# Summing and turning the modulation chunks four at a time in two projection stages

## The chip, the cores and the metric

One core of a Trainium2 chip runs the whole program. The metric is the device time of one execution in microseconds (us), as a median of several executions. TensorE is PE in the rows (its weight loads PEld), VectorE DVE, ScalarE ACT, GpSimd POOL, SyncE SP.

## What is computed

A two-layer network over 512 latent and 256 context rows of width 1024, followed by a second block; all in float32. Only the modulation matters here: for each layer a vector of six times 1024 numbers, once for the latent condition and once for the context condition, which shifts and scales the normalised rows and gates the two residual sums.

```python
silu_c = jax.nn.silu(c)
silu_cc = jax.nn.silu(c_ctx)
for i in range(DEPTH):
    ...
    sh1l, sc1l, g1l, sh2l, sc2l, g2l = [m[:, None, :] for m in jnp.split(silu_c @ ada_w[i] + ada_b[i], 6, axis=-1)]
    sh1c, sc1c, g1c, sh2c, sc2c, g2c = jnp.split(silu_cc @ ada_w[i] + ada_b[i], 6, axis=-1)
    h_lat = rmsnorm(x, norm1_w[i]) * (1.0 + sc1l) + sh1l
    h_ctx = rmsnorm(ctx, norm1_w[i]) * (1.0 + sc1c) + sh1c
    ...
    x = x + g1l * o_lat
```

## The kernel before

The program is a row of stages; each stage is a block that all engines enter and leave together, so a stage begins when the last engine of the one before is done. Weights come in chunks of 1024 x 512 through a ring of three slots, loaded by SP in a fixed order; SP waits for a slot to be free before it issues the next load. Every large product is made from a high and a low part of each operand (three matmuls, all at line 608); POOL and ACT cut the weights into these parts (lines 127, 128, 134).

The modulation is 24 chunks of 512 columns (12 for each layer). Four of them belong to `prologue`, 12 are spread over `ssd_project` and 8 over `project_qkv`. The class `Modulate` handles one chunk `i` at a time, with one PSUM bank for the products and one for all that follows:

- `products` (line 440, PE): the two condition vectors, padded to 32 columns, times the chunk. Eight matmuls of 32 columns; the k-th goes to column group k mod 4, that is to PSUM partitions 0, 32, 64 or 96, so that four groups hold partial sums. It waits for `copied` of the chunk before.
- `copy` (line 448, ACT): PSUM bank to SBUF (`part`).
- `sums` (line 454, PE): one matmul with `pick`, a 128 x 2 matrix of ones in the right rows, adds the four partial rows to two rows.
- `add` (line 461, DVE): adds the bias to the two rows (2 x 512).
- `turn` (line 468, PE): four transposes of 2 x 128.
- `file` (lines 479 and 483, DVE): copies the turned columns to `modc` if the chunk is one that is used as columns; for a scale also 1 + and times the norm weight.
- `store` (line 490, SP): at the stage's end the rows of chunks in `keep` go to DRAM.

`prepare` (lines 420 to 425, POOL) makes the padded conditions and `pick` at the stage's start; `start` (line 416, SP) loads the biases. In `ssd_project` the order on PE is written by hand: for n = 0 to 3 (the z part) four blocks b of 36 matmuls, with `products(n)` after b = 1, `sums(n)` after b = 2, `turn(n)` after b = 3; then 32 passes f (the x part), each of 48 matmuls and, from f = 1 to 24, six transposes of the pass before (line 955), with `products`, `sums` and `turn` of chunk 4 + f // 4 after passes f with f mod 4 = 1, 2, 3. A pass goes on to ACT (copy, line 1015), DVE (convolution, lines 1070 and 1074), ACT (silu, lines 1022 and 1023), PE (the transposes of line 955, behind the matmuls of the next pass) and DVE again (`file(f)` of the stage, lines 1055 and 1056).

In `project_qkv` PE does j = 0, 1, 2 (keys and values, first and second half of the queries) of four blocks b each, and then turns twelve tiles (`turn(n)`, lines 2996 and 2999); the modulation steps stand between these. DVE does norm and rotation of each part (`scale`, lines 3090 to 3102, and `rope`, lines 3112 to 3115) with the modulation's `add` and `file` between them, for instance

```python
            x = q[:, :, 0:HALF]
            scale(1, x, NL, 8, NT + NL)
            mod.file(dve, 2)
            rope(x, 0, 8, 0)
            rope(x, 0, 8, 1)
            mod.add(dve, 3)
```

## Time and profile before

| | us |
|---|---|
| median of 3 runs | 3552.27 |
| lowest, highest | 3546.49, 3552.39 |
| span of the profiled execution | 3548.8 |
| PE busy in it | 3138.1 (88%) |
| DVE, ACT, POOL busy in it | 1363.9, 986.9, 822.8 |
| `ssd_project`, first to last of PE's matmuls at line 608 | 69 to 547 |
| `project_qkv` | 1613.5 to 1735 |

The profiled execution has no time of its own but its span; the median stands 3.5 us above that span. The profile's page gives busy times over the whole span, so what a change in one stage is worth has to be read from that stage's own rows: start to start of neighbouring instructions on the engine that never idles, and the waits in square brackets.

### The profile page before, as it was taken

The page shows a single profiled execution, that of the slowest core. Times are in us where ns is not written, and L with a number is a line of the kernel's source. Part 1 is how long each engine was busy: PE and PEld are TensorE (multiplying, and loading weights), DVE is VectorE, ACT ScalarE, POOL GpSimd, SP SyncE. Part 2 cuts the span into 40 slices and gives each one's busy share as a digit, 9 for nine tenths or more (in the row PEclk, how much of TensorE's full clock was granted, in tenths as well). Part 3 has the DMA queues.
Part 4 walks back from the last instruction along what each step waited for, and adds up shares of the span by engine and source line. Part 5 has one row for each costly group of instructions (what it writes and reads, how often), then busy time and mean ns, then how long its engine had stood idle before and what let it go on. Part 6 is the DMA issues. An engine that isn't in the chain of part 4 may idle for free. (4 is left out here: it accounts for less than half of the span.)

```text
span 3548.8 us, 41092 instructions
## 1 busy us (share of the span) xinstructions
PE 3138.1 (88%) x16301; PEld 1978.1 (56%) x16301; DVE 1363.9 (38%) x2165; ACT 986.9 (28%) x2224; POOL 822.8 (23%) x574
## 2 busy tenths in 40 slices
PE   5999997878969999968899698887998996879998
PEld 3778885656723333326567233333776645668877
DVE  2128876774331111114664321113637743233311
ACT  3112225654132221223353211111343302332211
POOL 3333324660001101113101000000533101434432
PEclk8999999998979999989999799999999998899999
DMA  6444454433099999962303899998123133132231
GB/s 224 147 150 136 156 182 153 149 96 136 5 372 395 396 402 395 400 235 100 141 1 125 324 401 412 416 411 342 57 85 109 63 134 110 48 119 93 69 129 42
DMA packets 272074, 697.21 MB, mean 196 GB/s; under 512 B 16032, under 2 KB 62972, under 8 KB 269580
## 3 DMA queue, kind: packets, MB, share of 16 engines
q1 hardware_dynamic: 263104, 672.35, 50.2%
q0 software_dynamic: 6656, 16.78, 2.0%
q10 hardware_dynamic: 2124, 5.46, 0.4%
q8 instruction: 130, 2.13, 0.3%
q14 instruction: 60, 0.49, 0.0%
HBM read 647.30 MB, written 47.25 MB: 196 GB/s over the span
## 5 line engine op out<-in xcount | busy, mean ns | idle before, releaser
L608 PE MATMUL ps<-h_parts,weights_high 128*128 128x512 f32 (+3 forms) x2560 | 745.7, 377 | 29.1 <-PEq L258 17.6
L134 POOL TENSOR_TENSOR weights_low<-ring,weights_high 128x1024 fp32r<-128x1024 f32 (+1 forms) x205 | 499.1, 2438 | 712.0 <-ACT weights_high L127 701.9
L608 PEld LDWEIGHTS ps<-h_parts,weights_high 128*128 128x128 f32 (+2 forms) x2560 | 466.3, 190 | 139.1 <-POOL weights_low L134 26.6
L608 PE MATMUL ps<-h_parts,weights_low 128*128 128x512 f32 (+2 forms) x1280 | 479.5, 375 | 0.0
L1989 PE MATMUL ps<-area 128*32 128x512 f32 (+1 forms) x1632 | 285.9, 597 | 2.6 <-ACT area L2077 2.5
L608 PEld LDWEIGHTS ps<-h_parts,weights_low 128*128 128x128 f32 (+1 forms) x1280 | 242.5, 189 | 47.0 <-issue 0.8
L127 ACT ACTIVATE weights_high<-ring 128x1024 fp32r<-128x1024 f32 (+1 forms) x138 | 143.8, 1051 | 252.4 <-PE ps L608 233.3
L2187 PE MATMUL ps<-area 128*64 128x512 f32 x832 | 190.2, 610 | 20.0 <-ACT area L2267 7.0
L608 PE MATMUL ps<-weights_high,h_parts 128*128 128x512 f32 x608 | 197.6, 400 | 7.1 <-PEq L258 7.1
L1989 PEld LDWEIGHTS ps<-area 128*32 128x32 f32 (+1 forms) x1632 | 84.0, 124 | 189.1 <-issue 186.4
L1074 DVE SCALAR_TENSOR_TENSOR area<-area,param_columns 128x772 f32<-128x772 f32 x128 | 184.2, 1439 | 10.0 <-issue 0.4
L1989 PE MATMUL ps<-ring,area 128*32 128x512 f32 (+1 forms) x864 | 155.4, 595 | 0.1
L2187 PEld LDWEIGHTS ps<-area 128*64 128x64 f32 x832 | 69.6, 140 | 132.2 <-issue 130.6
L608 PEld LDWEIGHTS ps<-weights_high,h_parts 128*128 128x128 f32 x608 | 115.0, 189 | 47.2 <-issue 20.1
L1975 POOL DMA_INDIRECT summed_rows<-area,picked_half_rows x16 | 25.1, 1569 | 480.1 <-DVE area L2114 480.1
L608 PE MATMUL ps<-weights_high,y_parts 128*128 128x512 f32 x384 | 122.2, 398 | 6.9 <-DVE weights_low L1655 6.9
L608 PE MATMUL ps<-weights_low,h_parts 128*128 128x512 f32 x304 | 120.4, 396 | 0.0
L608 PE MATMUL ps<-weights_high,hidden_parts 128*128 128x512 f32 x352 | 112.5, 400 | 7.2 <-POOL weights_low L134 7.2
L2187 PE MATMUL ps<-ring,area 128*64 128x512 f32 x432 | 102.2, 620 | 18.0 <-DMA ring<-in_moe_w 5.8
L148 POOL CAST weights_high<-ring 128x1024 fp32r<-128x1024 f32 x18 | 20.6, 1147 | 410.6 <-DVE area L758 192.9
L1262 ACT ACTIVATE weight_parts<-ps,area 128x128 f32<-128x128 f32 x384 | 104.4, 391 | 32.4 <-PE ps L1189 32.1
L128 POOL CAST weights_high<-ring 128x1024 fp32r<-128x1024 f32 (+1 forms) x49 | 50.7, 1034 | 268.6 <-PE ps L608 268.4
(449 smaller groups left out, 4786.8 us busy)
## 6 DMA issues: line engine op xcount, KB each, us to landing
area<-in_moe_w SPq DMA_DIRECT2D x103, 2048.0 KB, 24.6
ring<-in_moe_w SPq DMA_DIRECT2D x54, 2048.0 KB, 25.4
weight_parts<-in_moe_w SPq DMA_DIRECT2D x35, 2048.0 KB, 24.6
ring<-in_ada_w SPq DMA_DIRECT2D x24, 2048.0 KB, 8.4
ring<-in_ssd_in_w SPq DMA_DIRECT2D x12, 2048.0 KB, 7.9
ring<-in_w_in SPq DMA_DIRECT2D x11, 2048.0 KB, 7.9
ring<-in_w_ffn_in SPq DMA_DIRECT2D x10, 2048.0 KB, 7.7
area<-x_dram SPq DMA_DIRECT2D x12, 1024.0 KB, 5.0
```

The lines of the kernel that those rows point to most:

```text
L127: return eng.activation(hi, src, ACT.Copy)
L128: return eng.tensor_copy(hi, src)
L134: pool.tensor_tensor(lo, views[k][:, ks, cols], hi, ALU.subtract).then_inc(self.low_p, 1)
L148: pool.tensor_copy(self.part(self.hi, m, ks, cols), src[:, ks, cols])
L608: mm = pe.matmul(out, a, b, start=start and n == 0, stop=stop and n == 2)
L1074: last = dve.scalar_tensor_tensor(c, pad[:, f % 2, j:j + width], col(env, "ssd_conv_w", j * 32 + f), c, ALU.mult, ALU.add)
L1262: last = act.activation(ex[:, u % 3, d, h * P:(h + 1) * P], spread_at(u, d)[:, h * P:(h + 1) * P], ACT.Exp, bias=nacum[:, c, hh:hh + 1])
L1975: pool.indirect_dma_start(out=halves, out_offset=at(env.spots, e), in_=y[e % 2], in_offset=None, compute_op=ALU.add).then_inc(added, 16)
L1989: mm = pe.matmul(ps[i * n:(i + 1) * n, bank, :], x, w, start=first, stop=last, skip_group_check=True)
L2187: mm = pe.matmul(ps[i * L:(i + 1) * L, bank, :], x, w, start=first, stop=last, skip_group_check=True)
```

## The change

A new class `ModulateFours` takes the place of `Modulate` in `ssd_project` (12 chunks, three fours) and `project_qkv` (8 chunks, two fours). `products` is as before. `copy` puts the four chunks of a four side by side into a buffer of 4 x 512. `sums` works on a four: `pick` is padded to 32 columns and four matmuls put the sums of the four chunks at PSUM partitions 0, 32, 64 and 96 of one bank. `add` is one instruction of 128 x 512, `turn` four transposes of 128 x 128, and `file` picks the columns of all four chunks. Since only two of each 32 rows carry values, POOL clears the whole row buffer first, and SP's bias loads (and whatever SP has behind them) wait for that. Of the 16 row stores 8 are left: `keep` is (2, 5) in place of (2, 3, 4, 5). The places of the steps move too, and in `project_qkv` `prepare` moves to the front of POOL's work. `prologue` keeps the old class.

```diff
+class ModulateFours:
+    def start(self, sp):
+        sp.wait_ge(self.cleared, 1)
+        for i, (layer, c) in enumerate(self.chunks):
+            sp.dma_start(self.place(i), self.env.ins["ada_b"][layer, c * HALF:(c + 1) * HALF]
...
+    def prepare(self, pool):
+        pool.memset(self.rows, 0.0).then_inc(self.cleared, 1)
+        pool.memset(self.cond, 0.0)
+        pool.memset(self.pick, 0.0)
+        pool.drain()
+        pool.tensor_copy(self.cond[:, :, 0:2], self.env.cond[:])
+        for j in range(4):
+            pool.tensor_tensor(self.pick[:, 0:2], self.pick[:, 0:2], self.env.ident[:, 32 * j:32 * j + 2], ALU.add)
+            pool.drain()
...
+    def copy(self, act, i):
+        act.wait_ge(self.env.mod_used, self.m0 + i + 1)
+        if i >= 4:
+            act.wait_ge(self.summed, i // 4)
+        act.activation(self.part[:, i % 4, :], self.env.ps[:, self.banks[0], :], ACT.Copy).then_inc(self.copied, 1)
+
+    def sums(self, pe, b):
+        if b >= 1:
+            pe.wait_ge(self.filed, b)
+        pe.wait_ge(self.copied, 4 * b + 4)
+        for j in range(4):
+            mm = pe.matmul(self.env.ps[32 * j:32 * j + 32, self.banks[1], :], self.pick, self.part[:, j, :], start=True, stop=True,
+                           skip_group_check=True)
+        mm.then_inc(self.summed, 1)
...
+    def turn(self, pe, b):
+        pe.wait_ge(self.added, b + 1)
+        for j in range(4):
+            s = slice(j * P, (j + 1) * P)
+            tr = pe.transpose(self.env.ps[:, self.banks[1], s], self.rows[:, b, s], self.env.ident[:])
+        tr.then_inc(self.turned, 1)
...
@@ ssd_project
-        mod = Modulate(env, st, [(0, c) for c in range(4, 12)] + [(1, c) for c in range(4)], (6, 7), keep=(2, 3, 4, 5))
+        mod = ModulateFours(env, st, [(0, c) for c in range(4, 12)] + [(1, c) for c in range(4)], (6, 7), keep=(2, 5))
...
-                    elif b == 2:
-                        mod.sums(pe, n)
-                    elif b == 3:
-                        mod.turn(pe, n)
+            mod.sums(pe, 0)
...
+                if f == 0:
+                    mod.turn(pe, 0)
                 if n < mod.n:
                     if f % 4 == 1:
                         mod.products(pe, n, at[n])
-                    elif f % 4 == 2:
-                        mod.sums(pe, n)
-                    elif f % 4 == 3:
-                        mod.turn(pe, n)
+                    elif f % 16 == 14:
+                        mod.sums(pe, n // 4)
+                    elif f % 16 == 15:
+                        mod.turn(pe, n // 4)
...
-            for n in range(nz):
-                mod.add(dve, n)
-                mod.file(dve, n)
+            mod.add(dve, 0)
+            mod.file(dve, 0)
...
@@ project_qkv
-                if m == CUTS:
+                if m == ahead:
                     mod.prepare(pool)
...
-                    if j >= 1 and b % 2 == 0:
-                        mod.sums(pe, 2 * j - 2 + b // 2)
+                    if (j, b) == (2, 2):
+                        mod.sums(pe, 0)
                     if b % 2 == 1 and j + b > 1:
-                        if j >= 1:
-                            mod.turn(pe, 2 * j - 2 + b // 2)
                         mod.products(pe, 2 * j - 1 + b // 2, at_mod[2 * j - 1 + b // 2])
```

PE at the end of `project_qkv`, from the last `turn` inside the loop over j to the end of the stage. Before (468 is `turn` of a chunk, 454 `sums`, 440 `products`, 2996 and 2999 the stage's own turns):

```order
L468 MATMUL ps<-identity,area 128x2 x4
L440 MATMUL ps<-ring,area 32x512 x8
L2996 MATMUL ps<-identity,area 64x128 x24
L454 MATMUL ps<-area 2x512
...
L468 MATMUL ps<-identity,area 128x2 x4
L440 MATMUL ps<-ring,area 32x512 x8
L454 MATMUL ps<-area 2x512
L468 MATMUL ps<-identity,area 128x2 x4
L2999 MATMUL ps<-identity,area 128x128 x16
```

After (551 is `products`, 566 `sums` of a four, 582 `turn` of a four, 3111 and 3114 the stage's own turns):

```order
L551 MATMUL ps<-ring,area 32x512 x8
L3111 MATMUL ps<-identity,area 64x128 x24
L582 MATMUL ps<-identity,area 128x128 x4
...
L3114 MATMUL ps<-identity,area 128x128 x8
L551 MATMUL ps<-ring,area 32x512 x8
L3114 MATMUL ps<-identity,area 128x128 x8
L566 MATMUL ps<-area 32x512 x4
L3114 MATMUL ps<-identity,area 128x128 x8
L582 MATMUL ps<-identity,area 128x128 x4
```

The last two chunks' chains of products, sums and turn no longer stand ahead of the last four of the stage's own turns; the second four is summed and turned between and behind them.

DVE in `project_qkv`, from the first scaling of the second half of the queries on. Before (461 is `add`, 479 and 483 `file`, 3102 the scaling, 3112 the first step of a rotation):

```order
L3090 TENSOR_TENSOR area<-area 128x2048
...
L461 TENSOR_TENSOR area<-ps,area 2x512
...
L3102 TENSOR_TENSOR area<-area 128x512 x4
L479 COPY modulation_columns<-ps 128x2x4
L483 SCALAR_TENSOR_TENSOR modulation_columns<-modulation_columns,param_columns 128x2x4
L3112 TENSOR_TENSOR area<-area 128x256 x4
```

After (575 is `add`, 596 the copy in `file`, 3075 the copy of a turned tile):

```order
L575 TENSOR_TENSOR area<-ps,area 128x512
L3204 TENSOR_TENSOR area<-area 128x2048
...
L3215 TENSOR_TENSOR area<-area 128x512 x4
L3225 TENSOR_TENSOR area<-area 128x256 x4
...
L596 COPY modulation_columns<-ps 128x2x4 x2
L3075 COPY area<-ps 128x512
L575 TENSOR_TENSOR area<-ps,area 128x512
```

One `add` stands ahead of the last scaling, and no modulation step is left between it and the last rotation.

POOL at the start of `ssd_project`, ahead of its first cut of weights. Before:

```order
L420 MEMSET area 128x256
L421 COPY area<-identity 128x2
L423 COPY area<-conditions 128x8x2
L425 TENSOR_TENSOR area<-area,identity 128x2 x3
L128 CAST weights_high<-ring 128x512
```

After:

```order
L530 MEMSET area 128x1536
L531 MEMSET area 128x256
L532 MEMSET area 128x32
L534 COPY area<-conditions 128x8x2
L536 TENSOR_TENSOR area<-area,identity 128x2 x4
L128 CAST weights_high<-ring 128x512
```

A clearing of 1536 columns, one of 32 and a fourth addition come in ahead of the first cut; a copy of two columns goes.

## Rows read from the trace of the kernel before

**Rows 1.** The page's first line.
```profile
span 3548.8 us, 41092 instructions
```

**Rows 2.** Windows: PE, PEld, DVE, ACT, POOL busy; granted clock; DMA share; GB/s.
```profile
69.00:547.00 478.00, 476.67 (x2573) 377.24 (x2574) 258.12 (x243) 84.94 (x169) 168.88 (x96) 0.99 0.46 156
1613.50:1709.80 96.30, 95.75 (x440) 67.30 (x440) 41.11 (x83) 21.38 (x30) 27.59 (x16) 0.98 0.44 156
1709.80:1735.00 25.20, 20.59 (x204) 11.58 (x201) 19.23 (x42) 9.11 (x16) 0.00 (x0) 1.00 0.69 252
```

**Rows 3.** Timeline of PE in the z part: products; one chunk's sums between matmuls.
```profile
97.16 1.92 PE L440 MATMUL ps<-ring,area 128*32 128x512 f32 x16
...
107.02 0.40 PE L608 MATMUL ps<-weights_low,h_parts 128*128 128x512 f32 x1
107.25 0.40 PE L608 MATMUL ps<-weights_high,h_parts 128*128 128x512 f32 x1
107.58 1.02 PE L454 MATMUL ps<-area 128*2 128x512 f32 x2
108.53 0.50 PE L608 MATMUL ps<-weights_high,h_parts 128*128 128x512 f32 x1
108.86 0.39 PE L608 MATMUL ps<-weights_low,h_parts 128*128 128x512 f32 x1
```

**Rows 4.** Timeline of PE: first x pass; then stage transposes and a chunk's turn.
```profile
229.93 0.70 PE L608 MATMUL ps<-h_parts,weights_high 128*128 128x512 f32 x2 [0.72 <-ACT area L1007]
...
269.04 0.82 PE L955 MATMUL ps<-identity,area 128*128 128x128 f32 x6
269.79 0.41 PE L468 MATMUL ps<-identity,area 2*128 2x2 f32 x4
270.12 0.73 PE L608 MATMUL ps<-h_parts,weights_high 128*128 128x512 f32 x2
```

**Rows 5.** Clearings on POOL by form; timeline of PE at the start of `ssd_project`.
```profile
L1727 POOL MEMSET area<- 128x512 f32 x1 | 0.5, 525 | 178.5 <-POOLq L258 178.5
L420 POOL MEMSET area<- 128x256 f32 x3 | 0.9, 312 | 16.2 <-POOLq L258 16.2
...
68.96 1.11 PE L608 MATMUL ps<-h_parts,weights_high 128*64 128x512 f32 x2 [8.14 <-POOL weights_low L134]
```

**Rows 6.** Timeline: silu's second half on ACT, transposes on PE, convolution on DVE.
```profile
270.80 6.29 DVE L1074 SCALAR_TENSOR_TENSOR area<-area,param_columns 128x772 f32<-128x772 f32 x4
277.66 0.40 ACT L1023 ACTIVATE area<-area 128x256 f32<-128x256 f32 x1
278.69 0.82 PE L955 MATMUL ps<-identity,area 128*128 128x128 f32 x6
...
408.24 0.40 ACT L1023 ACTIVATE area<-area 128x256 f32<-128x256 f32 x1
408.77 0.84 PE L955 MATMUL ps<-identity,area 128*128 128x128 f32 x6
...
528.05 4.31 DVE L1074 SCALAR_TENSOR_TENSOR area<-area,param_columns 128x772 f32<-128x772 f32 x4
```

**Rows 7.** Timeline of SP at the end of `ssd_project`: the row stores.
```profile
553.77 2.44 SPq L490 DMA_DIRECT2D mod_rows_dram<-area  x8
```

**Rows 8.** Waits of DVE from 1678 to 1709 us: total, times, longest.
```profile
DVE area L461 <- PE ps L454: 7.4, 2, 3.8
DVE modulation_columns L479 <- PE ps L468: 3.7, 2, 2.6
```

**Rows 9.** Timeline of the end of `project_qkv` and the first matmul behind it.
```profile
1708.35 2.29 DVE L3090 TENSOR_TENSOR area<-area 128x2048 f32<-128x2048 f32 x1
...
1728.47 0.42 DVE L3115 TENSOR_TENSOR area<-area 128x256 f32<-128x256 f32 x1
...
1731.97 2.00 PE L2999 MATMUL ps<-identity,area 128*128 128x128 f32 x16
...
1735.02 1.42 PE L2790 MATMUL ps<-area 64*128 64x256 f32 x6 [1.05 <-PEq L258]
```

More of the change, by code:

```diff
@@ L493, in kept, with __init__, end, place @@
         sp.wait_ge(self.stored, 16 * sum(c // 2 in self.keep for _, c in self.chunks))
+class ModulateFours:
+    def __init__(self, env, st, chunks, banks, keep=()):
+        self.env, self.chunks, self.banks, self.keep = env, chunks, banks, keep
+        self.n = len(chunks)
+        self.fours = self.n // 4
+        self.cond, self.pick = st.sb("padded_conditions", [P, KD, 32]), st.sb("pick_rows", [P, 32])
+        self.part = st.sb("partial_rows", [P, 4, HALF])
+        self.rows = st.sb("mod_rows", [P, self.fours, HALF])
+        self.ready, self.bias_in, self.copied = st.sem("conditions_ready"), st.sem("bias_in"), st.sem("partials_copied")
+        self.summed, self.added, self.turned = st.sem("fours_summed"), st.sem("bias_added"), st.sem("fours_turned")
+        self.filed, self.stored, self.cleared = st.sem("columns_filed"), st.sem("mod_stored"), st.sem("rows_cleared")
+        self.m0 = env.mods
+        env.mods += self.n
+    def end(self, i):
+        self.env.ring_.ends.append([(self.env.mod_used, self.m0 + i + 1)])
+        return len(self.env.ring_.ends) - 1
+    def place(self, i):
+        return self.rows[32 * (i % 4):32 * (i % 4) + 2, i // 4, :]
+    def start(self, sp):
+        sp.wait_ge(self.cleared, 1)
+        for i, (layer, c) in enumerate(self.chunks):
+            sp.dma_start(self.place(i), self.env.ins["ada_b"][layer, c * HALF:(c + 1) * HALF]
+                         .partition_broadcast(2)).then_inc(self.bias_in, 16)
+    def prepare(self, pool):
[7 more added lines that the diff above has]
+            pool.drain()
+        pool.drain().then_inc(self.ready, 1)
+    def products(self, pe, i, k):
+        env, bank = self.env, self.banks[0]
+        if i == 0:
+            pe.wait_ge(self.ready, 1)
+        else:
+            pe.wait_ge(self.copied, i)
+        env.ring_.wait(pe, k)
+        w = env.ring_.view(k, KD, HALF)
+        for q in range(KD):
+            j = 32 * (q % 4)
+            mm = pe.matmul(env.ps[j:j + 32, bank, :], self.cond[:, q, :], w[:, q, :], start=q < 4, stop=q >= 4,
+                           skip_group_check=True)
+        mm.then_inc(env.mod_used, 1)
+    def copy(self, act, i):
[9 more added lines that the diff above has]
+            mm = pe.matmul(self.env.ps[32 * j:32 * j + 32, self.banks[1], :], self.pick, self.part[:, j, :], start=True, stop=True,
+                           skip_group_check=True)
+        mm.then_inc(self.summed, 1)
+    def add(self, dve, b):
+        if b == 0:
+            dve.wait_ge(self.bias_in, 16 * self.n)
+        dve.wait_ge(self.summed, b + 1)
+        rows = self.rows[:, b, :]
+        dve.tensor_tensor(rows, self.env.ps[:, self.banks[1], :], rows, ALU.add).then_inc(self.added, 1)
+    def turn(self, pe, b):
[4 more added lines that the diff above has]
+        tr.then_inc(self.turned, 1)
+    def file(self, dve, b):
+        env = self.env
+        dve.wait_ge(self.turned, b + 1)
+        turned = env.ps[:, self.banks[1], :].rearrange("p (k r) -> p r k", r=P)
+        for i in range(4):
+            layer, c = self.chunks[4 * b + i]
+            q = {0: 0, 1: 1, 3: 2, 4: 3}.get(c // 2)
+            if q is None:
+                continue
+            dst = env.modc[:, q, :, 4 * (c % 2):4 * (c % 2) + 4]
+            dve.tensor_copy(dst, turned[:, 32 * i:32 * i + 2, :])
+            if q in (1, 3):
+                dve.drain()
+                a = env.col_at["norm1_w" if q == 1 else "norm2_w"] + layer * KD + 4 * (c % 2)
+                dve.scalar_tensor_tensor(dst, dst, 1.0, env.cols[:, a:a + 4].unsqueeze(1).broadcast_to([P, 2, 4]), ALU.add, ALU.mult)
+        dve.drain().then_inc(self.filed, 1)
+    def store(self, sp):
+        for i, (layer, c) in enumerate(self.chunks):
+            if c // 2 in self.keep:
+                sp.wait_ge(self.added, i // 4 + 1)
+                sp.dma_start(self.env.mod_dram[layer, :, c * HALF:(c + 1) * HALF], self.place(i)).then_inc(self.stored, 16)
+    def kept(self, sp):
+        sp.wait_ge(self.stored, 16 * sum(c // 2 in self.keep for _, c in self.chunks))
@@ L1061, in _ @@
                 n = nz + f // 4
-                if f % 4 == 0 and f > 0:
-                    mod.file(dve, n - 1)
-                if f % 4 == 3:
-                    mod.add(dve, n)
+                if f % 16 == 0 and f > 0:
+                    mod.file(dve, n // 4 - 1)
+                if f % 16 == 15:
+                    mod.add(dve, n // 4)
                 dve.wait_ge(out, g0 + 2 * f + 2)
@@ L3024, in _ @@
             turn(1)
-            mod.sums(pe, 4)
+            mod.turn(pe, 0)
+            mod.products(pe, 5, at_mod[5])
             turn(2)
             turn(3)
-            mod.turn(pe, 4)
-            mod.products(pe, 5, at_mod[5])
             turn(4)
             turn(5)
-            mod.sums(pe, 5)
+            mod.products(pe, 6, at_mod[6])
             turn(6)
             turn(7)
-            mod.turn(pe, 5)
-            for i in (6, 7):
-                mod.products(pe, i, at_mod[i])
-                mod.sums(pe, i)
-                mod.turn(pe, i)
-            for n in range(8, 12):
-                turn(n)
+            mod.products(pe, 7, at_mod[7])
+            turn(8)
+            turn(9)
+            mod.sums(pe, 1)
+            turn(10)
+            turn(11)
+            mod.turn(pe, 1)
         @block.scalar
```

44 lines of the change are left out of this document (16 added, 28 removed).

## The prediction, made before the changed kernel ran

> **What bounds the kernel now.** I read the page first, then the stretches of the two changed stages, then the timeline of PE inside them, and last the other engines where PE waits. From 69 to 547 us, all of `ssd_project`'s matmuls, PE is busy 476.67 of 478.00 us at a granted clock of 0.99 [rows 2]; the next engine, DVE, is busy 258.12. So whatever is taken out of PE's row there shortens the stage, until the next chain is late. From 1613.5 to 1709.8 (`project_qkv`, the three parts) PE is again busy 95.75 of 96.30 us. Its last 25.20 us are different: PE is busy 20.59 us and DVE 19.23 [rows 2], and the last of the stage's own turns, 16 records at 1731.97, starts only when the last rotation on DVE, at 1728.47, and two chunks' chains are through [rows 9]. So that tail is bound by DVE and by hand-overs. The stages follow one another with a meeting of all engines, so I take what is won in one stage to be kept by the rest of the program.
>
> **Sums.** I read PE's timeline from start to start. Two matmuls of line 608 in a row start 0.23 us apart (107.02, 107.25); the sums start 0.33 after the matmul ahead, the next matmul 0.95 after the sums (107.58 to 108.53), and the one behind that 0.33 later again [rows 3]. So each edge costs 0.10 more than a plain step, and sums that stand alone cost 0.95 + 0.20 = 1.15 us. Where they follow other small work the edges are paid already: 0.95. What do four sums side by side cost? The row of products is the nearest: 16 records over four column groups in 1.92 us, against 2 records in 1.02 us for the single sum [rows 3]. Were nothing side by side, 16 records would take eight times the single sum, some 7.6 us. Four deep in each group fits the row, so two deep (four matmuls, 8 records) should take what one sum takes now. I use 0.95 or 1.15 for a four; the other end, nothing side by side, is 4 x 0.95 = 3.8.
>
> The Trainium skill (TensorE: Matmul & The Clock Gate, section Part 3: Packing small matmuls, row/col tiling) gives less than that: three column tiles of 32 x 512 measured 2.38 times as fast as one by one. By it, as an estimate, four sums would take about 1.25 times one; 0.24 us more for each of the five fours, 1 us in all. The products' row here is nearer to four times, and the sum goes by that row.
>
> **Turns.** Four small transposes take 0.33 us start to start (269.79 to 270.12), 0.53 when they stand alone. Six full ones take 0.75 (269.04 to 269.79), 0.125 each, so four full ones 0.50 [rows 4].
>
> **`ssd_project`, z part.** Four sums go: 4 x 1.15 = 4.6. Three turns go: 3 x 0.53 = 1.6. The fourth turn stood where PE then waited 0.72 us for ACT's last evacuation before the first x pass [rows 4]: going, it wins nothing, and the four's sums (0.95) stand in the same gap and cost nothing. Gain 6.2.
>
> **x part.** Eight sums go, six of them behind transposes: 6 x 0.95 + 2 x 1.15 = 8.0. Two fours come: 0.95 + 1.15 = 2.1. Gain 5.9. Turns: six behind transposes and one alone, 6 x 0.33 + 0.53 = 2.5; the eighth lies behind PE's last matmul and is off the path. One turn of a four comes, 0.5 (the last again off the path). Gain 2.0. The first four's turn is put behind the first pass, and DVE now files it ahead of its first convolution: turn and hand-over 0.75 us, two copies and a drain 0.5, less what ACT's copy takes anyway. PE waits there for the silu of that pass now, so the delay shows: I take a loss of 0.85, between 0 and 1.3.
>
> Is the next chain late then? PE's transposes of a pass wait for that pass's silu. In the pass after a turn, silu ended at 278.06 and PE came at 278.69, 0.6 us later; in the pass of the products 408.64 and 408.77, no more than the hand-over [rows 6]. A pass without modulation takes PE about 9.3 us, and the chain from its last matmul through copy, convolution and silu 9.0 (269.04 to 278.06 [rows 4, 6]). The slack is per pass and does not add up, so the gains stand, narrowly.
>
> **Start of the stage.** PE's first matmul at 68.96 has waited 8.14 us, at the end for POOL's first low part [rows 5]; all of `prepare` lies on that path. Clearing takes 312 ns for 256 columns and 525 for 512, so 0.83 ns a column and 1.38 us for 1536. The clearing of `pick` and the fourth addition come on top and a small copy goes; from the 312 ns of the smaller clearing I put the three at 0.2 to 0.3 together. Loss 1.6, at least the 1.38 and at most 3 if DVE's own clearing at the same time is in the way. SP's twelve bias loads wait for that clearing and the next ring load waits behind them; but that load also waits for POOL's first cut, and its slot is needed tens of us later: nothing.
>
> **End of the stage.** Eight stores take SP 2.44 us of issue behind the last feature store [rows 7]; four go. That wins up to 1.2, or nothing if the feature store lands last. I take 0.6.
>
> Stage: 6.2 + 5.9 + 2.0 - 0.85 - 1.6 + 0.6 = 12.25 us won.
>
> **`project_qkv`.** Up to the third part's evacuation four sums (1.15 each) give way to one: 3.45. The turns beside products cost 0.33 each, four of them, and one waited 0.5 more. PE's loop so ends some 4.9 us sooner. DVE can follow: between 1678 and 1709 us it waited 7.4 and 3.7 us for sums and turns of chunks [rows 8], 11.1 us that go. So the last scaling starts at 1703.45 in place of 1708.35. From there to the end of the last rotation (1728.89) DVE takes 20.54 us [rows 9]; the gaps that two adds, two files and a third add leave between its steps sum to 3.3 us, so 17.2 remain: 1720.65, 8.25 us sooner. Behind it stand two stage turns (half of the 16 records in 2.00 us, 1.0), the sums of the second four (1.0), two turns (1.0), four full transposes (0.6), two columns filed on DVE (1.2) and the meeting (0.4): 5.2 us, where before 6.1 lay between 1728.89 and the next stage's 1735.02 [rows 9]. Gain 9.1, of which I take 8.8 for hand-overs not seen. `prepare` grows to some 3.5 us and moves ahead of POOL's third cut, which PE needs about 15 us later: covered. The last ring loads go out sooner, not later.
>
> **Sum.** 12.25 + 8.8 = 21.05 us. Against the profiled span: 3548.8 [rows 1] to 3527.8. The median stands 3.5 above the span, so 3552.27 - 21.05 = 3531.2.
>
> **Rivals.**
> 1. DVE does not follow in `project_qkv`: its chain is late by something else (a ring load, ACT's queue), and only PE's 4.9 us count there. For: DVE has 11 us of waits that could hide others. Against: those waits name only sums and turns. 17.1 us won: 3535.
> 2. The change does not do what it says: the four sums run one after another. Each costs 2.85 more at five places, all but part of the first on the path: 14 us back, 7 won: 3545. Against it stands the products' row.
> 3. Slower: the convolution chain takes over in the x part. Its slack is 0.1 to 0.6 us a pass. The same four steps on DVE take 6.29 us where POOL cuts weights beside them and 4.31 where it doesn't [rows 6]. If PE's shorter passes move the cuts so that the whole chain (the first step too) is hit longer, each of 24 passes is late: at 0.9 us a pass the gain is gone, at 1.2 us the kernel takes 28.8 - 21 = 8 us more: 3560. Against: POOL starts a cut when PE ends a pass, so both move together. The Trainium skill (SBUF — State Buffer, section Who interferes with whom) says why it can happen at all: a VectorE instruction with two SBUF inputs contends with a GpSimd instruction that reads SBUF.
> 4. What is won is given back later, in a stage bound by its weight stream: 3550. Against: no load of a later stage starts before these stages end but for the ring's three slots.
>
> **Chances.** Forecast 0.72; rival 1 0.13; rival 2 0.05; rival 3 0.05; rival 4 0.05. A measurement of this kernel can tell about 0.2%, 7 us, from no change. Faster by more: 0.72 + 0.13 + a part of rival 2, 0.87; within: 0.08; slower: 0.05. Range: the lower end from the bounds (start at 1.4, first convolution hidden, end of stage 1.2, tail in full: 24 us) and 4 us of spread between runs, 3524; the upper end takes in rival 1 and the same spread, and comes near rival 2: 3543.
>
> **What would show it.** PE from its first matmul to its last in `ssd_project` shorter by about 13 us, its start 1.6 us later within the stage; a four's sums 0.95 us from start to next start; transposes of line 955's kind waiting no more than before except in the second pass; `project_qkv` 8 to 9 us shorter, with DVE's waits for sums gone; every later stage of its old length. A four's sums near 3.8 us would mean rival 2; waits of PE for silu of 0.5 us or more in most passes, rival 3.

## The result, and the profile after

The changed kernel took 3520.99 us (median of 4 runs, 3519.04 to 3523.30), beside 3551.17 (median of 4) for the kernel before on the same chip. The ratio on record is 0.9919, 95% interval 0.9906 to 0.9933; the two medians divided give 0.9915. Timed again in five rounds it took 3521.66 us beside 3549.63, with the same ratio and interval: 28.0 us faster. The prediction was 3531.2, range 3524.0 to 3543.0. The sign was right, and so was the mechanism in the two changed stages; the time lies 3 us below the range.

The page of the changed kernel, its first line and its busy row, answers to [rows 1]:

```profile
span 3521.5 us, 40919 instructions
...
PE 3112.1 (88%) x16241; PEld 1969.6 (56%) x16241; DVE 1351.5 (38%) x2150; ACT 984.0 (28%) x2224; POOL 822.0 (23%) x578
```

PE's busy time fell by 26.0 us and the span by 27.3. The windows of the two changed stages (columns as in [rows 2]) show that PE still bounds both, except in the last 20 us of `project_qkv`:

```profile
70.75:540.00 469.25, 462.95 (x2538) 374.82 (x2538) 252.60 (x240) 84.36 (x170) 169.34 (x96) 0.99 0.46 159
1595.75:1688.00 92.25, 92.22 (x440) 66.94 (x442) 43.40 (x78) 21.85 (x31) 27.07 (x18) 0.98 0.45 162
1688.00:1708.00 20.00, 16.52 (x180) 9.98 (x176) 16.90 (x41) 8.37 (x14) 0.00 (x0) 1.00 0.87 317
```

In the timeline of PE, a four's sums, at the end of the z part and behind a pass's transposes in the x part, are these (start, duration). They answer to [rows 3]:

```profile
224.49 0.40 PE L725 MATMUL ps<-weights_high,h_parts 128*128 128x512 f32 x1
224.81 1.07 PE L566 MATMUL ps<-area 128*32 128x512 f32 x8
225.98 0.70 PE L725 MATMUL ps<-h_parts,weights_high 128*128 128x512 f32 x2
...
371.35 0.82 PE L1069 MATMUL ps<-identity,area 128*128 128x128 f32 x6
372.09 1.06 PE L566 MATMUL ps<-area 128*32 128x512 f32 x8
373.09 0.73 PE L725 MATMUL ps<-h_parts,weights_high 128*128 128x512 f32 x2
```

Eight records (four sums) take 1.06 us, where one sum of two records took 1.02. Start to start it is 1.00 in the x part (372.09 to 373.09), where one sum took 0.95. So the four run side by side.

What the stretches took, from the start of one stage to the start of the next, in two profiles of the kernel before and two of the changed one:

| stretch (start in the first profile of before) | before, us | changed, us | difference of the means |
|---|---|---|---|
| setup, `prologue` (0) | 65.1, 64.9 | 65.3, 64.3 | -0.2 |
| `ssd_project` (65.1) | 492.6, 492.2 | 478.6, 478.3 | -14.0 |
| `ssd_scan` (557.6) | 274.7, 273.7 | 271.7, 271.6 | -2.5 |
| output, first MoE, norm (832.3) | 781.3, 780.6 | 780.2, 778.7 | -1.5 |
| `project_qkv` (1613.6) | 121.4, 122.2 | 112.3, 112.9 | -9.2 |
| attention and its `project_add` (1735.0) | 219.5, 220.2 | 220.0, 220.2 | +0.2 |
| second MoE (1954.5) | 515.1, 514.1 | 518.7, 521.0 | +5.3 |
| up to the third `project_add` (2469.6) | 474.3, 475.5 | 473.2, 475.2 | -0.7 |
| from there to the end (2943.9) | 604.9, 604.0 | 601.6, 601.5 | -2.9 |
| sum | 3548.8, 3547.3 | 3521.5, 3523.6 | -25.5 |

The two stages that the change touches won 23.2 us; the prediction had 21.05. The rest of the program, whose code is the same, moved by up to 5 us a stretch, in both directions, and much of that comes back in a second profile. The prediction had said that every later stage would keep its length. The experiments therefore ask what moves stages that nobody changed.

### The profile page after: what moved, and what is told of

Its sections match the earlier page's. It is cut to its first block and busy times, and to the rows that moved or that the text cites. A ratio compares the mean times of both kernels' runs of the same rounds, so it can differ in the third digit from the quotient of the medians.

```text
span 3521.5 us, 40919 instructions
## 1 busy us (share of the span) xinstructions
PE 3112.1 (88%) x16241; PEld 1969.6 (56%) x16241; DVE 1351.5 (38%) x2150; ACT 984.0 (28%) x2224; POOL 822.0 (23%) x578
```

## Experiments: the two stages alone, and the same kernel again

Theory A: the two stages' own gain is all there is, and the rest is spread between executions. Theory B: the change wins elsewhere too. The two kernels once more, and each stage's new class alone.

> The kernel before, unchanged, timed and profiled once more. Theory A (the two stages' own gain is about 23 us in the spans, and what the whole kernel won beyond that, 4 us of span and 7 us of the medians, is spread between executions): the medians of the two copies may differ by 1 to 4 us, and in the new profile the stages that the change does not touch differ from the first profile by up to 3 or 4 us each, in both directions, while project_qkv and ssd_project agree within 0.5 us. Theory B (the change wins 28 to 30 us, and 5 to 7 of them in stages that it does not touch): the untouched stages agree within 0.5 us each and sum to the same within 1 us.

> The changed kernel, unchanged, timed against the kernel before in five rounds. Theory A: a gain of 23 to 26 us, nearer to the two stages' 23.2 than the 30.2 of the medians so far. Theory B: 28 to 31 us again. Its profile gives the untouched stages' lengths once more: by A they differ from the first profile of the changed kernel by as much as those differ from the kernel before.

```diff
@@ ssd_project alone (the second line stays as it was in project_qkv)
-        mod = Modulate(env, st, [(0, c) for c in range(4, 12)] + [(1, c) for c in range(4)], (6, 7), keep=(2, 3, 4, 5))
+        mod = ModulateFours(env, st, [(0, c) for c in range(4, 12)] + [(1, c) for c in range(4)], (6, 7), keep=(2, 5))
```

> ModulateFours in ssd_project alone, project_qkv as before. Theory A (a stage's gain stays what it is, whatever the rest does): ssd_project 478.6 us long as in the changed kernel, project_qkv 121.4 as before, and the kernel 14 us faster. Theory B (something beyond the two stages gains): 17 to 20 us faster if it hangs on ssd_project. By the record ahead of the result it was 12.25.

> ModulateFours in project_qkv alone, ssd_project as before. Theory A: project_qkv 112.3 us long as in the changed kernel, ssd_project 492.6 as before, and the kernel 9 us faster; with the run of ssd_project alone the two gains sum to that of the whole change within 3 us. Theory B: 12 us or more, or a sum of the two that misses the whole by over 4 us. By the record ahead of the result it was 8.8.

| | median, us | ratio to before, 95% | `ssd_project` | `project_qkv` |
|---|---|---|---|---|
| before again | 3550.82 | 1.0007, 0.9998 to 1.0016 | 492.2 | 122.2 |
| changed again | 3521.66 | 0.9919, 0.9906 to 0.9933 | 478.3 | 112.9 |
| `ssd_project` alone | 3533.80 | 0.9953, 0.9940 to 0.9967 | 477.3 | 125.7 |
| `project_qkv` alone | 3540.04 | 0.9969, 0.9957 to 0.9981 | 492.5 | 112.5 |

The parts add up: 15.8 and 9.6 are 25.4 us, the whole is 28.0, and the intervals are wider than what lies between. Each stage's own gain is the same alone and together, within about 1 us. But neither theory fits the rest. The whole change's 28.0 us lie in the 28 to 31 of B and outside the 23 to 26 of A. The second MoE took 518.7 and 520.4 us in the two half kernels, 514 to 515 in both profiles of before. The last stretch took 602.3 and 601.7 in them, 604.9 and 604.0 before. That is too regular for spread (A), and it comes with either half, so it is no gain of a certain edit (B).

One thing is the clock's. In the kernel with `ssd_project` alone, `project_qkv`, not touched there, took 4 us more. Its end shows why (windows; the last columns are the granted clock, the DMA share and GB/s), beside the end of that stage in the kernel before:

```profile
1594.18:1708.00 113.82, 111.77 (x598) 76.75 (x598) 55.82 (x115) 28.65 (x42) 27.61 (x16) 0.98 0.48 171
1708.00:1719.85 11.85, 8.74 (x42) 4.45 (x42) 4.61 (x10) 1.79 (x3) 0.00 (x0) 0.71 0.41 157
...
1727.00:1734.98 7.98, 5.39 (x41) 2.66 (x40) 3.88 (x9) 1.79 (x4) 0.00 (x0) 1.00 0.53 203
```

The granted clock was 0.71 there, a mix of 1.2 and 2.4 GHz, behind a stretch in which PE was 98% busy at 0.98; in the kernel before it was 1.00 to the stage's end, though PE had been as busy ahead of it (110.95 of 113.45 us). So a fall of the clock that lands in another place goes with up to 4 us of one stage. Why it landed there is not shown.

## Experiments: PE's code loads

The page of the kernel before counts the DMA traffic by kind:

```profile
q8 instruction: 130, 2.13, 0.3%
q14 instruction: 60, 0.49, 0.0%
```

130 loads of 16 KB on one queue, 60 of 8 KB on another. The trace has 33,357 instructions of PE, so 257 for each of the 130; the other four engines have 7735, so 129 for each of the 60. By these counts the first queue brings PE's code and the second that of the others, 64 bytes an instruction. The change takes 135 instructions out of PE's row, so behind it each load falls at another instruction. Theory C is that the unchanged stages move because these loads do. Theory D is that the clock's falls, which go with the moments at which stages start, do it all. Padding tests C: instructions that only wait, put where PE waits anyway, move the loads and change no other work.

```diff
@@ setup, on PE (242 waits in the kernel before, which are 121 instructions; 270 in the changed one, 135)
+            for _ in range(242):
+                pe.wait_ge(masks, 2)
             pe.wait_ge(masks, 2)
             pe.wait_ge(loaded, 16 * (len(pieces) + 1))
```

> The kernel before with 121 more instructions on PE that only wait for something long there, in the 12 us in which PE waits for the first landing. PE's code arrives in loads of 16 KB, one for 256 of its instructions; the padding shifts where they fall, and from project_qkv on puts them where the changed kernel has them. Nothing else changes. Theory C (part of what the change won beyond its two stages is the place of PE's code loads): the project_add near 2944 us, whose reload of two tiles met a code load in both profiles of the kernel before (68.9 and 68.6 us) and not in those with the change (67.0 to 67.1), takes 67.0 here, the tile reload lands 4 us after its issue and not 5.2, and the stages behind it take the lengths of the changed kernel (48.68 to 47.6, 249.2 to 250.7); the MoE stage near 1955 us goes from 514 or 515 to 518 or more. Theory D (the untouched stages differ by the clock's drops alone, which follow the moments at which stages start): nothing of this changes, 68.6 to 68.9 again. Either way ssd_project and project_qkv stay at 492.4 and 121.4 to 122.2, and the median within 4 us of the kernel before.

> The changed kernel with 135 more waiting instructions on PE at the same place: as many as the change takes out, so from project_qkv on PE's code loads stand at the same instructions as in the kernel before. Theory C: the project_add near 2920 us takes 68.6 to 68.9 in place of 67.0, the stages behind it go back to the lengths of the kernel before (47.6 to 48.6, 250.7 to 249.2), the MoE stage near 1928 us goes back from 519 or 521 to about 515. Theory D: the lengths of the changed kernel stay. Either way ssd_project stays at 478.5 and project_qkv at 112.3 to 112.9.

```diff
@@ ssd_project, on GpSimd, in the kernel before
+            for _ in range(4):
+                pool.memset(junk, 0.0)
+                pool.drain()
             mod.prepare(pool)
             ring.cut(pool, blocks, views)
```

> The kernel before with four clearings of 512 columns on POOL (drained) put ahead of ssd_project's first cut: that stage starts its matmuls some 2.2 to 2.8 us later, and every stage behind it does, while no instruction of PE is added. Theory D (lengths of untouched stages hang on the moments at which they start, through the places at which PE's clock falls to its lower level): ssd_scan leaves its 273.7 to 274.7 by 1 us or more, and stages behind it shift too, so that the kernel loses visibly more or less than the 2.5 us. Theory C alone: all later stages of the lengths of the kernel before, 2.5 us lost in all. It also prices what stands ahead of the first cut: each us there is one us of the kernel.

The `project_add` near 2944 us loads two tiles of 512 KB while PE idles. This is its DMA view in the kernel before, padded before, and padded changed, from 2990 to 3008, 2996 to 3014 and 2964 to 2984 us (each kind of code load with packets, MB and share of the 16 DMA engines' time; then the two tiles, with the median us from issue to landing):

```profile
q8 instruction: 1, 0.02, 0.3%
q14 instruction: 1, 0.01, 0.2%
area<-in_mem SPq DMA_DIRECT2D x2, 512.0 KB, 5.2
```

```profile
q14 instruction: 1, 0.01, 0.1%
area<-in_mem SPq DMA_DIRECT2D x2, 512.0 KB, 4.1
```

```profile
q8 instruction: 1, 0.02, 0.5%
area<-in_mem SPq DMA_DIRECT2D x2, 512.0 KB, 5.1
```

Where one of PE's code loads runs beside it, the tiles land 5.1 to 5.2 us after their issue; where none does, 4.1, and 4.0 in the changed kernel. The stage's windows follow (before, padded before, changed, padded changed):

```profile
2943.86:3012.78 68.92, 50.35 (x208) 40.71 (x208) 16.48 (x34) 17.65 (x41) 9.60 (x4) 0.85 0.29 99
...
2949.85:3017.04 67.19, 49.93 (x208) 40.50 (x208) 16.44 (x34) 17.59 (x41) 9.60 (x4) 0.87 0.29 101
...
2919.88:2986.93 67.05, 49.83 (x208) 40.41 (x208) 16.41 (x34) 17.54 (x40) 9.59 (x4) 0.87 0.29 100
...
2917.55:2985.91 68.36, 50.10 (x208) 40.50 (x208) 16.48 (x34) 17.65 (x40) 9.61 (x4) 0.85 0.27 99
```

Padding alone turns the kernel before into 67.2 and the changed one into 68.4: theory C, in both directions. All sixteen profiles of this work bear it out: in the five with a load of PE beside the two tiles the stage takes 68.4 to 69.0 us, in the eleven without 66.8 to 67.5. Here 1.3 to 1.9 of the change's 27 us were no merit of the change. The stages behind follow partly. The one from 3028 us on takes 48.7 us before, 47.7 with padding, 47.6 changed and 48.9 with padding, as expected of C. The long one near 3160 us goes from 249.2 to 250.5 in the kernel before with padding, as expected, but to 251.5, not back to 249.2, in the padded changed kernel. So the lengths there hang on more than the load's place.

The second MoE took 521.7 us in the padded kernel before and 515.2 in the padded changed one, as expected of C. With PE's loads where the kernel before has them it took 513.5 to 515.2 us in five profiles, so C fits. It is not settled all the same: with PE's loads where the changed kernel has them it took 518.7 and 521.0 us in that kernel, but 517.4, 517.0 and once 515.4 with other edits (DVE padded, the serial sums and `prepare` later, below). That stage reads its weights at a DMA share of 0.98 to 0.99, and what moves it by 5 us stays open.

One expectation was missed: `project_qkv` took 124.2 us in the padded kernel before and not 121.4 to 122.2. The granted clock fell in its last 9.24 us, to 0.82, as it did with `ssd_project` alone. What sets the place of such a fall stays open.

The kernel before with a later start took `ssd_project` 495.1 us, 2.7 more, and 273.8 in the scan and 69.0 near 2944: these two did not move by where they began. Moments alone do not do it, so D falls for these stages. The long one near 3160 us did move, from 249.2 to 250.2, with PE's loads in place. The median of this kernel was 3552.15 beside 3548.28 (ratio 1.0007 to before, 0.9997 to 1.0017). The medians of the padded kernels were 3552.35 beside 3548.28 (1.0008, 0.9999 to 1.0018) and 3522.27 (0.9923, 0.9907 to 0.9940).

## Experiments: the scan, and DVE's code loads

The scan's 2.5 us did not follow PE's padding (275.3 and 270.6 us). The scan is a chain of short steps between PE and DVE, so the loads of the other engines were the next suspect. First every engine was padded in the setup, then DVE and PE alone.

> The changed kernel with instructions that only wait put into the setup on every engine: 81 on PE, 18 on DVE, 3 on ACT, 4 on SP, 125 on GpSimd, so that at the start of ssd_scan each engine stands at the same place in its 8 or 16 KB of code as in the kernel before. Theory C (the scan's 2 to 3 us are made by code loads of the other engines too, which fell at other steps): ssd_scan goes from 270.6 to 271.7 back to 273.7 to 275.3, scan to norm together from 1050 to 1052 back to 1054 to 1056. Theory D (something else in how that stage starts: the clock, what POOL and DVE have left over from ssd_project): it stays at 270 to 272.

> The kernel before with 175 waiting instructions on PE, 110 on DVE, 125 on ACT, 124 on SP and 3 on GpSimd in the setup: at the start of ssd_scan each engine stands at the same place in its code loads as in the changed kernel. Theory C: ssd_scan 270.5 to 272.5 in place of 273.7 to 275.3. Theory D: unchanged. ssd_project itself stays at 492 us within 1 us by both, since it is bound by PE's own stream with nothing else near.

```diff
@@ setup, on DVE alone (220 waits in the kernel before, which are 110 instructions; 36 in the changed one, 18)
+            for _ in range(220):
+                dve.wait_ge(masks, 1)
             for t in range(tiles):
                 dve.wait_ge(turned, t + 1)
```

> The kernel before with 110 waiting instructions on DVE alone, in the 12 us in which all engines wait for the first landings. DVE then stands at the start of ssd_scan at the same place in its code loads as in the changed kernel; PE's, ACT's and the others' loads stay. Theory C-DVE (the scan's 2 to 4 us come from DVE's own code loads): ssd_scan 270 to 272.5 in place of 273.7 to 275.3, and the median 2 to 6 us under the kernel before although nothing else changed. Theory C-PE (they come from PE's loads): ssd_scan stays at 273.6 to 275.3 and the median within 3 us.

> The changed kernel with 18 waiting instructions on DVE alone, as many as it has fewer than the kernel before by the start of ssd_scan. Theory C-DVE: ssd_scan goes from 270.6 to 271.7 up to 273.7 or more. Theory C-PE: it stays at 270 to 272.

> The changed kernel with 81 waiting instructions on PE alone, as many as it has fewer than the kernel before by the start of ssd_scan. Theory C-PE: ssd_scan goes from 270.6 to 271.7 up to 273.7 or more. Theory C-DVE: it stays at 270 to 272. If it stays in this run and in the one with DVE alone, it takes both or one of the other engines.

`ssd_scan` took 273.9 us in the changed kernel with all padded and 270.1 in the kernel before with all padded: swapped. (Four of these kernels have one time each: 3523.08 and 3548.12 us with all padded, 3521.51 for the changed kernel with DVE and 3522.44 with PE padded.) The windows of the scan in the kernel before, the kernel before with DVE padded, the changed kernel, that with DVE padded and that with PE padded:

```profile
557.62:832.28 274.66, 214.27 (x1122) 161.23 (x1122) 204.21 (x372) 171.92 (x593) 153.10 (x176) 0.90 0.43 138
...
557.02:827.08 270.06, 208.97 (x1122) 157.58 (x1122) 203.38 (x372) 171.48 (x593) 153.46 (x176) 0.92 0.44 141
...
543.84:815.53 271.69, 208.51 (x1122) 156.25 (x1122) 203.07 (x372) 171.23 (x592) 153.21 (x176) 0.92 0.44 140
...
542.55:816.19 273.64, 212.92 (x1122) 160.43 (x1122) 203.75 (x372) 171.50 (x592) 152.90 (x176) 0.91 0.44 139
...
542.90:814.26 271.36, 207.07 (x1122) 155.14 (x1122) 203.15 (x372) 171.75 (x592) 153.34 (x176) 0.93 0.44 140
```

DVE's padding swaps the scan by itself and PE's does nothing: it is the place of things in DVE's code. The timeline shows where it bites. In the kernel before DVE stands still ahead of its step at 633.39 (in square brackets the idle time ahead and what ended it):

```profile
632.17 0.80 DVE L1394 TENSOR_TENSOR area<-area 128x256 f32<-128x256 f32 x1
633.39 0.42 DVE L1396 TENSOR_TENSOR area<-ps,area 128x256 f32<-128x256 f32 x1 [0.43 <-issue]
633.51 1.05 POOL L1295 TENSOR_TENSOR area<-area 128x512 f32<-128x512 f32 x1
633.73 1.38 DVE L1369 TENSOR_TENSOR weight_parts<-weight_parts 128x512 f32<-128x512 f32 x1
...
635.92 1.10 PE L1215 MATMUL ps<-area,weight_parts 128*128 128x64 f32 x8 [1.72 <-DVE weight_parts L1371]
```

With DVE padded it does so earlier in the scan, and that step runs on without a gap (each line number is 2 higher, by the two lines of the padding):

```profile
594.12 0.42 DVE L1398 TENSOR_TENSOR area<-ps,area 128x256 f32<-128x256 f32 x1 [0.43 <-issue]
...
631.65 0.79 DVE L1396 TENSOR_TENSOR area<-area 128x256 f32<-128x256 f32 x1
632.52 0.42 DVE L1398 TENSOR_TENSOR area<-ps,area 128x256 f32<-128x256 f32 x1
...
632.86 0.73 DVE L1371 TENSOR_TENSOR weight_parts<-weight_parts 128x512 f32<-128x512 f32 x1
633.00 1.49 POOL L1297 TENSOR_TENSOR area<-area 128x512 f32<-128x512 f32 x1
...
634.40 1.10 PE L1217 MATMUL ps<-area,weight_parts 128*128 128x64 f32 x8 [0.72 <-DVE weight_parts L1373]
```

It is the same pattern in the changed kernel, gap early, and in the changed kernel with DVE padded, gap late. DVE stands 0.43 us without waiting for anything that the profile shows. Counted over all of DVE's instructions in the traces, this gap stands ahead of the 704th in the kernel before, the 704th and 960th with DVE padded, the 576th and 832nd in the changed kernel and the 704th in that with DVE padded: always 64 past a multiple of 128, the number that 8 KB hold.

Early in the scan it costs nothing: one step later DVE's starts agree with those of the kernel before within 0.1 us again. At the late place it costs more than itself. POOL's step at 633.51 now starts ahead of DVE's at 633.73, and that one takes 1.38 us in place of 0.73; PE's next wait is 1.72 us in place of 0.72. It reads so in both profiles of the kernel before and in the two padded changed kernels with the gap at the late place. The mean granted clock of the stage is lower there too (0.90 and 0.91 in place of 0.92 and 0.93). That is the first 1.0 us; how the rest of the 2 to 4 comes was not taken apart. Timed, the kernel before with DVE padded took 3545.58 us beside 3549.47: 3.9 us less by the medians, as expected of C-DVE, but 0.9993 by the ratio on record (0.9984 to 1.0002), which takes in no change. The swap is shown by the profiles and not by the times.

## Experiments: side by side, and prepare

```diff
@@ ModulateFours.sums, with a pick of [P, 4, P] whose part j has its two columns at 32 j
-            mm = pe.matmul(self.env.ps[32 * j:32 * j + 32, self.banks[1], :], self.pick, self.part[:, j, :], start=True, stop=True,
-                           skip_group_check=True)
+            mm = pe.matmul(self.env.ps[:, self.banks[1], :], self.pick[:, j, :], self.part[:, j, :], start=j == 0, stop=j == 3)
```

> The changed kernel with each four's sums made one after another: a pick of 128 columns for each chunk, that puts its rows at partitions 32 j, and four accumulating matmuls of full width; all else alike (the clearing of the wider pick takes some 0.6 us more at each stage start). Theory of the record: a four side by side takes as long as one sum did, 0.95 to 1.06 us, so serial ones take four times that, 3.8 us in place of 1.0, five times: 3 fours in ssd_project, 2.8 us more each, 1 to 2 us of the first hidden behind ACT's last evacuations: ssd_project 7 to 9 us longer than 478.5, project_qkv 4 to 6 longer than 112.5, the kernel 12 to 14 us slower than the changed one. Rival: the columns of a pass are cheap at full width too (PE streams 512 columns whatever the width, and the price of a sum is the hand-over): under 5 us in all.

The sums of one four in that kernel:

```profile
224.33 3.60 PE L568 MATMUL ps<-area 128*128 128x512 f32 x8
227.36 1.03 PE L726 MATMUL ps<-h_parts,weights_high 128*128 128x512 f32 x2
```

3.03 us start to start, against 1.00 where nothing else hides a part. `ssd_project` took 486.2 us (7.8 more), `project_qkv` 117.9 (5.3 more) and the kernel 3532.66 (0.9952, 0.9936 to 0.9969), 11 us more than the changed one. About 0.9 us of it is no matter of the sums: POOL makes a wider `pick`, and PE's first matmul comes 6.4 us after the start of `ssd_project` in place of 5.5. Five times 2.03 us are the other 10. (By the profiles the two stages lost 13.1 and other stages were shorter.) So being side by side is worth some 10 of the 28 us: without it the merging would still win, since the shared turns, adds and hand-overs remain. The expected 3.8 us for a serial four was too much; the 11 us lie just under the expected 12 to 14.

```diff
@@ ssd_project, on GpSimd
-            mod.prepare(pool)
-            ring.cut(pool, blocks, views)
+            for m in range(len(blocks)):
+                if m == 2:
+                    mod.prepare(pool)
+                ring.cut_high(pool, blocks, views, m)
+                pool.drain()
+                ring.cut_low(pool, blocks, views, m)
```

> The changed kernel with prepare moved in ssd_project: POOL makes the weight parts of the first two blocks first and clears and copies for the modulation behind them, ahead of the third block. Theory of the record (all of prepare, 3.4 us from 65.27 to 68.68 in the changed kernel's profile, lies on the path to PE's first matmul): that matmul starts 3.4 us after the stage's start and not 5.5 less than before by 0 to 1, the stage takes 475.1 us in place of 478.5, the kernel 3.4 us less: 3518. Rival: the third block is late by prepare's 3.5 us (POOL had 0.9 us of waiting before its fourth block), PE waits for it and for the padded conditions, and the stage wins 0 to 1 us.

The start of the stage, on PE and on POOL, in that kernel:

```profile
64.54 0.61 POOL L128 CAST weights_high<-ring 128x512 fp32r<-128x512 f32 x1 [1.13 <-POOLq L258]
...
66.61 1.12 PE L725 MATMUL ps<-h_parts,weights_high 128*64 128x512 f32 x2 [6.82 <-POOL weights_low L134]
...
69.99 1.38 POOL L530 MEMSET area<- 128x1536 f32 x1
```

PE's first matmul comes 2.1 us after the stage's start, where it came 5.5 after it in the changed kernel: the 3.4 us of `prepare`, as expected. The stage took 474.5 us, 3.9 less (expected: 475.1). The kernel took 3513.21 us beside 3549.66 (0.9897, 0.9881 to 0.9914). That is 8.4 us under the changed kernel, where 3.4 were expected. 3.9 of them are the stage; the other 4.5 lie in stages whose code is that of the changed kernel, the second MoE (515.4) first, and are not explained.

## Why the prediction was right where it was, and where it failed

**z part.** Predicted 6.2 won. From PE's first matmul to the first x pass: 68.96 to 229.93 before, 160.97 us; 70.75 to 225.98 after, 155.23. 5.7 won: right within 0.5.

**x part.** Predicted 5.9 + 2.0 - 0.85 = 7.05; from the first x pass to PE's last matmul it was 316.67 before (to 546.60) and 307.72 after (to 533.70): 8.95. Three terms were mis-sized. The passes show it, by the starts of their transposes; one of before, then the changed kernel's, the last one ending the pass with the second four's sums (372.09 above):

```profile
258.80 0.82 PE L955 MATMUL ps<-identity,area 128*128 128x128 f32 x6
...
254.87 0.82 PE L1069 MATMUL ps<-identity,area 128*128 128x128 f32 x6
264.03 0.85 PE L1069 MATMUL ps<-identity,area 128*128 128x128 f32 x6
273.18 0.82 PE L1069 MATMUL ps<-identity,area 128*128 128x128 f32 x6
...
381.61 0.82 PE L1069 MATMUL ps<-identity,area 128*128 128x128 f32 x6
```

A pass that had sums took 10.24 us before (258.80 to 269.04), one that had a turn 9.65 (269.04 to 278.69, [rows 4, 6]). The same passes take 9.16 and 9.15 now. So a sum behind transposes cost 1.08, where the sum of the prediction had 0.95, and a turn 0.50 where it had 0.33. What failed is "the edges are paid already": the distance to the next start leaves out what an instruction adds ahead of itself. The six transposes at 254.87 take 0.57 us to the next start, a large matmul at 255.44; the six at 258.80 in the kernel before took 0.74, with sums at 259.54 behind them. Both terms come out larger: 8 x 1.08 less two fours' 1.1 each is 6.4, seven turns' 3.5 less 0.4 is 3.1. The pass with the four's sums takes 10.26 (371.35 to 381.61), as the one with a single sum did.

The third term is the loss of 0.85 in the first pass, which was nothing, the low end of its range. From its start to the first transposes (229.93 to 247.61 before, 225.98 to 243.68 after) it is 17.68 and 17.70 us, though the first four's turn now stands between:

```profile
247.61 0.87 PE L955 MATMUL ps<-identity,area 128*128 128x128 f32 x6 [0.60 <-ACTq L1024]
...
243.68 0.87 PE L1069 MATMUL ps<-identity,area 128*128 128x128 f32 x6 [0.16 <-ACTq L1140]
```

PE already waited 0.60 us there for the silu; the turn takes the place of most of that wait. The three make 9.5 us and not 8.95: in two later passes PE waited 0.36 and 0.09 us for their silu (321.47, 468.77), so the chain that the prediction called narrow did come late there, and cost that much.

**Start and end.** 1.6 lost at the start, as predicted (5.48 against 3.90 us to the first matmul). At the end 11.02 us became 10.14, 0.9 won where I took 0.6 from 0 to 1.2. The stage won 14.0 us and not 12.25.

**`project_qkv`.** DVE follows PE, as forecast, and rival 1 falls. The start of the last scaling stands at 1685.99, 90.2 us behind the stage's start (94.8 before): 4.6 sooner where the prediction said 4.9. (Its terms there, 3.45, four times 0.33 and 0.5, add up to 5.3.) It waits for the evacuation of what PE made, and no longer for sums or turns. From there to the end of the last rotation it is 17.0 us, forecast 17.2. These are its first row and the stage's last matmuls:

```profile
1685.99 2.29 DVE L3204 TENSOR_TENSOR area<-area 128x2048 f32<-128x2048 f32 x1 [5.61 <-ACT area L3174]
...
1703.17 1.06 PE L3114 MATMUL ps<-identity,area 128*128 128x128 f32 x8 [1.81 <-DVEq L3248]
1704.16 1.06 PE L566 MATMUL ps<-area 128*32 128x512 f32 x8
1705.16 1.09 PE L3114 MATMUL ps<-identity,area 128*128 128x128 f32 x8
1706.09 0.61 PE L582 MATMUL ps<-identity,area 128*128 128x128 f32 x4
```

The tail behind the last rotation takes 5.0 us where the sum had 5.2. The stage won 9.2, predicted 8.8. Rival 2 falls by the 1.06 us above, rival 3 by the pass lengths (11.19 in both, then 9.16 against 10.24). Rival 4, that a stage bound by its weight stream gives the gain back, falls as a whole; but the second MoE, with a DMA share of 0.98 to 0.99, did take 5.3 us more. A four took 0.05 us more than one sum (1.00 against 0.95), where the prediction's estimate beside its sum had 0.24 (and five times 0.24 is 1.2, not 1).

**What failed** is the step "I take what is won in one stage to be kept by the rest of the program", read as "every later stage of its old length". Unchanged stages moved by -2.5, -1.5, +5.3 and -2.9 us. For the scan the cause is shown (a stop of DVE that moves with its code), though only the first 1.0 us of the 2 to 4 is traced; for the stage near 2944 it is shown too (PE's code loads); for the second MoE it is not. Second, the base: I took 3552.27, a median of three runs, 3.5 above the span. Over later sets of 16, 19, 7 and 15 runs the kernel before had medians of 3549.63, 3548.28, 3549.66 and 3549.47. From 3549.6 the same gain of 21.05 gives 3528.5, and the low end of the range (24 won, 4 of spread) 3521.6, still 0.6 above the measured time. The range failed by the same two steps: its 4 us of spread stood for runs of one kernel and held nothing for unchanged stages, and the base's 3 us were in neither end. Of the 10 us by which the time was missed, some 3 are the base, 2 the two stages' terms, and 2.3 the sum of the unchanged stages by the profiles (25.5 less 23.2). The last 2.5 stay open: the medians differ by 28.0 us where the profiled spans differ by 25.5.

## What to carry to other kernels

Price a small instruction between large ones by the length of a whole pass with and without it, not by the distance from its start to the next: that distance missed 0.13 us for a sum and 0.17 for a turn here. A change that takes instructions out moves every later code load of that engine, and unchanged stages can answer by 2 to 4 us in either direction, so a gain below that is not the change's before a kernel with only padding has been seen. Work that an engine needs late (a clearing for a later step) belongs behind the first pieces that another engine waits for: 3.4 us here for the move of `prepare`.

## What the runs showed of the hardware

Four sums of 32 columns side by side took 1.00 us start to start, one alone 0.95, four one after another (each 128 columns wide) 3.03. By the Trainium skill (TensorE: Matmul & The Clock Gate, section Part 3: Packing small matmuls, row/col tiling) three column tiles were 2.38 times as fast as one by one. Here four were 3.0 times as fast, which agrees: 0.79 of the number of tiles there, 0.76 here. That a four still takes hardly longer than one is no contradiction, since one after another each took 0.76 us and not 0.95.

Beside a single code load of 16 KB, 0.3% of the DMA engines' time in an 18 us window, two tiles of 512 KB landed 1.1 us later. A stop of 0.43 us on DVE in a chain of short hand-overs was worth 2 to 4 us of the scan, or nothing, by where in the chain it fell; at the costly place it let a step of POOL start ahead of one of DVE, which then took 1.38 us in place of 0.73.
